# One streaming-encoder layer on one core: five reorderings of loads, sums and the final normalisation

## The chip, the cores and the metric

The kernel runs on one core of a Trainium2 chip. The metric is device time in microseconds (us); before the change three runs gave 1188.85, 1189.27 and 1189.97, median 1189.27.

## The reference, cut to what matters

For x of shape (1024, 2048), all in float32:

```
h    = rmsnorm(x) * norm_g
proj = h @ w_in                                  # 2048 x 5120
ya   = gelu(ua) * (W_s layernorm(gelu(va)) + b)  # chunked spatial gating
yb   = windowed attention(q, k, v) with sinks and relative bias
yc   = (trailing mean of 2/4/8/16 tokens - token) @ w_pool * c_scale
mix  = [ya*silu(ga), yb*silu(gb), yc*silu(gc)]
out  = rmsnorm(x + mix @ w_out) * final_g
```

## The kernel before, in words

**Tiling.** Both projections are cut into seven products of 1024 output columns, called pairs: five on w_in (PAIR_F, TA, TB, C, A, numbers 0 to 4) and two on w_out (PAIR_O, PAIR_U, 5 and 6). Each pair is computed by a Strassen-like scheme of seven block products of 512 rows by 1024 inner by 512 columns; each product takes two steps, c = 0 and 1. There are 98 steps, numbered 0 to 97. Steps 70 to 77 alternate between the pairs: O, O, U, U, O, O, U, U. Steps 78 to 87 are the rest of O and 88 to 97 the rest of U.

**One step.** TensorE multiplies 48 times, 128x128 by 128x512: four PSUM banks (st = 0 to 3), four operand slots (k = 0 to 3), and three matmuls each, because every float32 operand is split into a high and a low part in the fast float32r format (`three`). The high part of a weight tile is a ScalarE copy (`split_hi`), the low part a VectorE subtraction (`split_lo`), both one step ahead: while TensorE is in step J (we call that period J) these engines split the weights of step J + 1. VectorE also forms the sums of weight blocks (`weight_sum`), adds PSUM banks to the result quadrants (`add_chain`), and does what the layer needs between.

**Order.** Each engine runs a loop over the steps that is written out by hand, and inside an iteration strictly in order of the text. Engines meet at semaphores. SyncE (SP) issues nearly all DMAs; its iteration n does the stores of sums (`save_jobs`), weight loads (`pair_loads`), then the four slot loads of step n + 2 (`load_s`), each behind the release of its slot, then `result_loads` (mixed values, residual rows). All of SP's DMAs are on one queue. GpSimd issues, on its own queue, the saves of the first pair's operand splits (`save_first`, steps 6 to 13), on whose landing the slot loads of step 14 wait.

**Row tiles.** `ROWS_LOADED` says in which iteration one of eight 1 MB tiles of x is loaded, for the sums of squares that ScalarE takes one iteration later (`square_rows`). For an iteration below 12 the load stands ahead of `load_s(n + 2)`, from 12 on behind it. The split of weights is the first thing in ScalarE's iteration, `square_rows` nearly the last.

**Pooling.** In periods 55 to 63 VectorE's `pool_half(u)` computes a trailing mean into the tile `aux` (signal `pool_in`), TensorE's `pool_map(u)` multiplies it into the PSUM bank E[1] behind the first bank of step 56 + u, and `pool_gate(u)` empties that bank (`c_done`). `pool_map(u)` waits for `pool_half(u)` and for `pool_gate(u - 1)`.

**The end.** `finish_first` (one function on ScalarE, one on VectorE) takes the root of the first 512 rows' mean squares and scales their four 1 MB result tiles, eight instructions on each engine. SP then stores the four tiles (line 890) in iteration 96, which it reaches after the last slot loads. In the same iteration, ahead of these stores, `result_loads` loads the last 1 MB of residual rows (line 833) into the one buffer `residual`. In period 97 VectorE adds it (`add_residual`, line 1629), and only behind that, in its program order, come the last bank additions, squares, roots and scalings of the second 512 rows, and their stores (lines 896, 902 and 943).

```
if J == step(PAIR_O + 1, 12):       # = 96, the last thing of the iteration
    finish_first()
```

Of the kernel before, what the change touches and what calls it, by code (L numbers as in the profile page):

```python
# [8 lines left out]
ALU = mybir.AluOpType  # L9
# [27 lines left out]
CHUNKS = PAIRS * STEPS  # L37
# [18 lines left out]
def step(p, g):  # L56

    return 2 * SEQUENCE.index((p, g // 2)) + g % 2
# [100 lines left out]


ROW_TILES = HALVES * ST
ROWS_LOADED = {5: 0, 6: 1, 7: 2, 9: 3, 10: 4, 11: 5, 13: 6, 15: 7}
AT_ROOT = (11, 17)
AT_ROWS = (13, 19)
AT_KV = (13, 18)
# [89 lines left out]
def build(nc, x, x_t, w_b, norm_g, ln_g, ln_b, w_s, b_s, sinks, rel_bias, one_hot, inv_count, w_pool,  # L255
# [8 lines left out]
    with ExitStack() as ctx:  # L264
# [276 lines left out]
        def _(sp):  # L541
# [143 lines left out]
            def pair_loads(n):  # L685

                p, j = at_step(n)
                first, second, third = BUFS[p]
                following = p + 1 < PAIRS
                if n == step(PAIR_O, 0) - 1:  # L690
                    split_done(n + 1)
                    load_w(BUFS[PAIR_O][0], PAIR_U, B21, 0)
                for c in range(2):
                    if p == PAIR_F:
                        if j == c:
                            split_done(2 + c)
                            load_w(second, p, B22, c)
                        if j == 7 + c:
                            sums_done(p, 5 + c)
                            load_w(first, p, B22, c)  # L700
                            split_done(8 + c)
                            load_w(third, p, B21, c)
                        if j == 9 + c:
                            split_done(10 + c)
                            load_w(first, p + 1, FIRST_BLOCKS[p + 1][1], c)
                        if j == 11 + c:
                            sums_done(p, 7 + c)
                            load_w(third, p + 1, FIRST_BLOCKS[p + 1][0], c)
                        if j == 12 + c:
                            split_done(n)  # L710
                            load_w(second, p + 1, FIRST_BLOCKS[p + 1][2], c)
                    elif p == PAIR_O:
                        if j == 0 and c == 1:
                            split_done(n + 1)
                            load_w(first, PAIR_U, B21, c)
                        if j == 2 + c:
                            split_done(n)
                            sums_done(p, 1 + c)
                            load_w(second, p, B22, c)
                        if j == 6 + c:  # L720
                            split_done(n)
                            load_w(third, p, B12, c)
                        if j == 9 + c:
                            sums_done(p, 5 + c)
                            load_w(second, p, B21, c)
                        if j == 10 + c:
                            split_done(n)
                            load_w(third, PAIR_U, B12, c)
                        if j == 11 + c:
                            sums_done(p, 7 + c)  # L730
                            load_w(second, PAIR_U, B11, c)
                        if j == 12 + c:
                            split_done(n)
                            load_w(first, PAIR_U, B22, c)
                    elif p == PAIR_U:
                        if j == c:
                            split_done(n)
                            load_w(first, p, B11, c)
                        if j == 6 + c:
                            split_done(n)  # L740
                            load_w(third, p, B12, c)
                        if j == 9 + c:
                            sums_done(p, 5 + c)
                            load_w(first, p, B21, c)
                    elif early(p):
                        if j == c:
                            split_done(n)
                            load_w(first, p, B22, c)
                        if j == 6 + c:
                            split_done(n)  # L750
                            load_w(third, p, B12, c)
                        if j == 9 + c:
                            sums_done(p, 5 + c)
                            load_w(first, p, B21, c)
                        if following and j == 10 + c:
                            split_done(n)
                            load_w(third, p + 1, FIRST_BLOCKS[p + 1][0], c)
                        if following and j == 11 + c:
                            sums_done(p, 7 + c)
                            load_w(first, p + 1, FIRST_BLOCKS[p + 1][1], c)  # L760
                        if following and j == 12 + c:
                            split_done(n)
                            load_w(second, p + 1, FIRST_BLOCKS[p + 1][2], c)
                    else:
                        if j == 8 + c:
                            split_done(n)
                            load_w(third, p, B21, c)
                        if following and j == 6 + c:
                            split_done(n)
                            load_w(second, p + 1, FIRST_BLOCKS[p + 1][0], c)  # L770
                        if following and j == 11 + c:
                            sums_done(p, 7 + c)
                            load_w(third, p + 1, FIRST_BLOCKS[p + 1][1], c)
                        if following and j == 12 + c:
                            split_done(n)
                            load_w(first, p + 1, FIRST_BLOCKS[p + 1][2], c)
# [71 lines left out]
            for n in range(CHUNKS):  # L848
# [33 lines left out]
                if n == AT_LAYER:  # L882
                    load_layer_constants()
                result_loads(n)
                if n == CHUNKS - 2:

                    for c, y, done, count in ((0, y11[PAIR_O], y_scaled, 4), (1, y12[PAIR_O], y_scaled, 8),
                                              (2, y11[PAIR_O + 1], y_normed, 4), (3, y12[PAIR_O + 1], y_normed, 8)):
                        sp.wait_ge(done, count)
                        sp.dma_start(out[0:HS, 512 * c:512 * c + 512].rearrange("(t r) d -> r t d", t=ST), y[:]  # L890
                                     ).then_inc(y_stored, 16)
# [56 lines left out]
        def _(sc):  # L948
# [300 lines left out]
            for J in range(TOTAL):  # L1249
# [3 lines left out]
                if J == 0:  # L1253
                    for k in range(4):
                        first_hi(1, k)
                        split_hi(1, (k,))
                elif J + 1 < TOTAL and J not in SUM_S3:
                    split_hi(J + 1)
                if 0 < J < STEPS - 1:
                    first_hi(J + 1, 0)  # L1260
                    if J in SUM_S3:
# [46 lines left out]
                    square_rows(ROWS_LOADED[J - 1])  # L1308
                if j == 2 * EARLY.index(Q_S2) + 1 and early(p) and p > PAIR_F:
                    copy_u(p, range(ST - 1))  # L1310
                if J == step(PAIR_O + 1, 12):
                    finish_first()
            last_square(0)
            last_square(1)
            second_root(0, 2, 2)
# [14 lines left out]
        def _(ve):  # L1330
# [141 lines left out]
            def weight_sums(n):  # L1472
# [9 lines left out]
                    if j in (11, 12):  # L1482
                        weight_sum(p, j - 4, j - 11, 1, 2, 1, ALU.subtract, (2, 2))
                elif p == PAIR_O:
                    if j == 1:
                        weight_sum(p, 1, 0, 2, 2, 1, ALU.subtract, (1, 1), (2, 1))
                    if j in (8, 9):
                        weight_sum(p, j - 3, j - 8, 2, 1, 2, ALU.subtract, (2, 2))
                    if j in (10, 11):
# [3 lines left out]
                    if j == 13:  # L1493
                        weight_sum(PAIR_U, 3, 1, 2, 2, 1, ALU.subtract, (1, 4), (2, 3))
                elif p == PAIR_U:
                    if j == 0:
                        weight_sum(PAIR_O, 2, 1, 2, 2, 1, ALU.subtract, (1, 1), (2, 1))
                    if j in (2, 3):
                        ve.wait_ge(lo_done, split_index(n, 1) + 1)
                        weight_sum(PAIR_O, j + 1, j - 2, 0, 1, 2, ALU.subtract, (1, 2))  # L1500
# [148 lines left out]
            def pool_half(u):  # L1649
# [6 lines left out]
                settle(ve.tensor_copy(pool_x[:, 0:HIST], hist[:, j, :]))  # L1656
                settle(ve.tensor_tensor(pool_x[:, HIST:HIST + HS], pool_src[half][:, j, :], rstd_row[half][:], ALU.mult))
                settle(ve.tensor_copy(hist[:, j, :], pool_x[:, HS:HS + HIST]))
                if u >= 1:
                    ve.wait_ge(pool_ready, u)  # L1660
                window = POOLS[j]
                src = pool_x
                for m in range(j + 1):
                    lo, by, dst = 2 ** (m + 1) - 1, 2 ** m, (pool_a, pool_b)[m % 2]
                    settle(ve.tensor_tensor(dst[:, lo:HIST + HS], src[:, lo:HIST + HS],
                                            src[:, lo - by:HIST + HS - by], ALU.add))
                    src = dst
                last = ve.scalar_tensor_tensor(out=aux[:], in0=src[:, HIST:HIST + HS], scalar=1.0 / window,
                                               in1=pool_x[:, HIST:HIST + HS], op0=ALU.mult, op1=ALU.subtract)
                if half == 0:  # L1670
# [101 lines left out]
            for n in range(CHUNKS):  # L1772
# [41 lines left out]
                    weight_sum(PAIR_U, 4, 1, 1, 0, 2, ALU.subtract, (0, 4))  # L1814
                if STEPS <= J + 1 < TOTAL:
                    split_lo(J + 1)
                if J in PIECE_OF and PIECE_OF[J] % 2 == 0:
                    query_lo(PIECE_OF[J])
                for k, gate in enumerate(GATES):
# [34 lines left out]
                    previous_values()  # L1854

                u = J - POOL_AT
                if 0 <= u < 8:
                    pool_gate(u)
                if 0 <= u + 1 < 8:
                    pool_half(u + 1)  # L1860
                if J == step(PAIR_A, 7):
                    ve.wait_ge(mixed_loaded[0], 16 * 4)
                    ve.wait_ge(y_gated, 7)
# [21 lines left out]
                for i, t in enumerate((step(PAIR_O, 8), step(PAIR_O, 11), step(PAIR_O, 13), step(PAIR_U, 5),  # L1885
                                       step(PAIR_U, 6), step(PAIR_U, 10))):
                    if J == t:
                        weigh(i)
                if J == step(PAIR_O + 1, 12):
                    finish_first()  # L1890

            add_chain(PAIRS - 1, Q_A22, (0, 1))
            second_root(0, 2, 2)
# [322 lines left out]
```

## Time and profile before

| | |
|---|---|
| median of three runs | 1189.27 us |
| profiled execution, device time | 1189.71 us |
| its span, first to last instruction | 1187.9 us |
| busy: TensorE / VectorE / ScalarE / GpSimd | 98% / 73% / 41% / 3% |
| moved by DMA | 355 MB, mean 299 GB/s |

Busy time is time in which an instruction of that engine ran. The span is the profiled execution's time less 1.8 us that lie around it. With TensorE at 98% a change can gain only in the few places where it waits, at the start, and in the 12 us after its last matmul.

### The profile page before, as it was taken

Reading aid. Unit: us, or ns where it says so; the run is one execution under the profiler, and the core shown is the slowest. Engines: PE = TensorE matmul, PEld = TensorE weight load, DVE = VectorE, ACT = ScalarE, POOL = GpSimd, SP = SyncE. Lnnn points to the kernel's source line nnn. Section 1 sums busy time; section 2 is a strip of 40 time slices with the busy share of each in tenths; the row PEclk is TensorE's granted clock in tenths of the full one; section 3 lists DMA queues with packets and bytes.
Section 4 is the critical chain, followed back from the end, with each engine's and each line's share of the span. In section 5 each row is a group of like instructions: output and inputs, shape, how many; then the busy total and the mean of one; then the engine's idle time right before and its main releaser. Section 6 shows DMA issues by size and latency. Waiting matters only on the chain.

```text
span 1187.9 us, 15646 instructions
## 1 busy us (share of the span) xinstructions
PE 1169.2 (98%) x5862; PEld 954.5 (80%) x5862; DVE 872.3 (73%) x1150; ACT 491.5 (41%) x863; POOL 37.5 (3%) x76
## 2 busy tenths in 40 slices
PE   9999999999999999999999999999999999999995
PEld 8878878888888888888888877778878888888884
DVE  5799939677777767888776797988777445586674
ACT  6375564524534333447333362423333432223235
POOL 0012100000000000000000000000000000000000
PEclk9999999999999999999999999999999999999998
DMA  9999999687864476996567686799997648896878
GB/s 349 418 375 415 394 416 346 203 308 286 320 226 160 163 268 243 347 341 202 190 231 261 206 336 232 255 323 363 420 412 302 248 175 342 321 413 226 310 280 326
DMA packets 103435, 354.98 MB, mean 299 GB/s; under 512 B 10656, under 2 KB 17856, under 8 KB 92224
## 3 DMA queue, kind: packets, MB, share of 16 engines
q1 hardware_dynamic: 98432, 336.15, 76.7%
q0 software_dynamic: 4928, 17.83, 3.7%
q8 instruction: 47, 0.77, 0.2%
q14 instruction: 28, 0.23, 0.0%
HBM read 282.37 MB, written 71.57 MB: 298 GB/s over the span
## 4 chain that ended last, share of the span: by engine, by line
PE 81%; DVE 9%; DMA 7%; issue 1%; SPq 1%; ACT 1%; POOL 0%; DVEq 0%; ACTq 0%
PE n_bank L1911 25%; PE n_bank L1912 25%; PE n_bank L1913 25%; DMA x_parts<-s_ring 3%; PE e_bank L2062 2%; DVE w_lo L1344 2%; PE t_bank L2090 2%; PE t_bank L2073 2%; DMA xc<-x_t_dram 2%; DVE w_b L1469 1%; DMA s_ring<-m_parts 1%; DMA s_ring<-x_parts 1%; DVE s_ring L1353 1%; DMA xa<-x_t_dram 1%; DVE va L1526 0%
## 5 line engine op out<-in xcount | busy, mean ns | idle before, releaser
L1006 ACT ACTIVATE w_hi<-w_b 128x1024 fp32r<-128x1024 f32 (+1 forms) x200 | 197.8, 1033 | 421.1 <-PE n_bank L1913 365.3
L1911 PE MATMUL n_bank<-s_ring,w_hi 128*128 128x512 f32 x896 | 357.5, 399 | 1.3 <-DMA s_ring<-x_parts 1.3
L1913 PE MATMUL n_bank<-s_ring,w_lo 128*128 128x512 f32 x896 | 349.0, 390 | 0.0
L1912 PE MATMUL n_bank<-s_ring,w_hi 128*128 128x512 f32 x896 | 349.0, 389 | 0.0
L1344 DVE TENSOR_TENSOR w_lo<-w_b,w_hi 128x1024 fp32r<-128x1024 f32 (+1 forms) x200 | 231.9, 1198 | 102.9 <-ACT w_hi L1006 102.7
L1911 PE MATMUL n_bank<-w_hi,s_ring 128*128 128x512 f32 x672 | 262.1, 390 | 2.0 <-DMA s_ring<-m_parts 0.9
L1913 PE MATMUL n_bank<-w_hi,s_ring 128*128 128x512 f32 x672 | 261.5, 389 | 0.0
L1912 PE MATMUL n_bank<-w_lo,s_ring 128*128 128x512 f32 x672 | 261.5, 389 | 0.0
L1911 PEld LDWEIGHTS n_bank<-s_ring,w_hi 128*128 128x128 f32 x896 | 168.2, 188 | 41.7 <-issue 2.5
L1913 PEld LDWEIGHTS n_bank<-s_ring,w_lo 128*128 128x128 f32 x896 | 168.2, 188 | 35.7
L1912 PEld LDWEIGHTS n_bank<-s_ring,w_hi 128*128 128x128 f32 x896 | 168.3, 188 | 35.3 <-issue 2.2
L1911 PEld LDWEIGHTS n_bank<-w_hi,s_ring 128*128 128x128 f32 x672 | 126.1, 188 | 30.9 <-DMA s_ring<-m_parts 2.4
L1913 PEld LDWEIGHTS n_bank<-w_hi,s_ring 128*128 128x128 f32 x672 | 126.1, 188 | 26.1
L1912 PEld LDWEIGHTS n_bank<-w_lo,s_ring 128*128 128x128 f32 x672 | 126.1, 188 | 25.9
L1469 DVE TENSOR_TENSOR w_b<-w_b,w_b 128x2048 f32<-128x2048 f32 x56 | 127.9, 2285 | 3.9 <-DMA w_b<-w_b_dram 3.7
L1701 DVE SCALAR_TENSOR_TENSOR probs<-e_bank,score_scale,bias 64x256 f32<-64x256 f32 x128 | 56.4, 481 | 81.0 <-PE e_bank L2062 80.6
L1240 ACT ACTIVATE probs<-probs,minus_max 128x129 f32<-128x129 f32 x128 | 50.0, 393 | 51.7 <-DVE minus_max L1712 51.7
L937 POOL COPY probs<-sink_sb 128x4 f32<-128x4 f32 x32 | 17.3, 540 | 517.9 <-ACT probs L1240 412.8
L1526 DVE TENSOR_TENSOR o<-n_bank,o 128x512 f32<-128x512 f32 x32 | 20.9, 686 | 16.5 <-PE n_bank L1913 16.0
L1526 DVE TENSOR_TENSOR u<-n_bank,u 128x512 f32<-128x512 f32 x32 | 21.0, 687 | 14.1 <-PE n_bank L1913 13.8
L2090 PEld LDWEIGHTS t_bank<-probs_t,v_prev 128*64 128x64 f32 x256 | 14.7, 136 | 11.7 <-issue 11.7
L1240 ACT ACTIVATION_READ_ACCUMULATOR probs<-probs,minus_max 128x1 f32 x128 | 23.9, 187 | 0.0
(210 smaller groups left out, 945.3 us busy)
## 6 DMA issues: line engine op xcount, KB each, us to landing
s_ring<-x_parts SPq DMA_DIRECT2D x224, 512.0 KB, 6.0
w_b<-w_b_dram SPq DMA_DIRECT2D x76, 1024.0 KB, 10.6
s_ring<-m_parts SPq DMA_DIRECT2D x96, 512.0 KB, 6.1
x_parts<-s_ring POOLq DMA_DIRECT2D x32, 512.0 KB, 11.4
x_parts<-s_ring SPq DMA_DIRECT2D x24, 512.0 KB, 14.5
m_parts<-stage SPq DMA_DIRECT2D x20, 512.0 KB, 8.6
rows<-x_dram SPq DMA_DIRECT2D x8, 1024.0 KB, 11.3
residual<-x_dram SPq DMA_DIRECT2D x6, 1024.0 KB, 9.5
```

Of the source, the lines that this page charges most:

```text
L1006: sc.activation(w_hi[:, J % 2, part], w_source(J)[:, part], ACT.Copy).then_inc(hi_done, 1)
L1240: sc.activation(part, part, ACT.Exp, bias=minus_max[:, b:b + 1], accum_out=row_sum[:, b:b + 1]).then_inc(exp_done, 1)
L1344: ve.tensor_tensor(w_lo[:, J % 2, part], w_source(J)[:, part], w_hi[:, J % 2, part].bitcast(F32), ALU.subtract).then_inc(lo_done, 1)
L1469: ve.tensor_tensor(out[:], a[:], b[:], op).then_inc(w_summed, 1)
L1526: ve.tensor_tensor(out[:, st, :], N[st][:], to[:, st, :], ALU.add).then_inc(y_added, 1)
L1701: last = ve.scalar_tensor_tensor(out=logits[rows, 2 * tl:2 * tl + 2, 0:P], in0=e_banks[rows, :, at:at + P], scalar=score_scale[rows, half, ...
L1911: pe.matmul(psum_out, stat[0], mov[0], start=first, stop=False)
L1912: pe.matmul(psum_out, stat[0], mov[1], start=False, stop=False)
L1913: return pe.matmul(psum_out, stat[1], mov[0], start=False, stop=last)
L2062: mm = pe.matmul(E[a][:, 256 * tl:256 * tl + WINDOW], q_part[rows, at:at + P], k_part[rows, q0:q0 + WINDOW], start=k == 0, stop=k == 2)
L2073: mm = pe.transpose(PT_bank[:, P * b:P * b + P], logits[:, b, 0:P], ident[:])
L2090: mm = pe.matmul(O_bank[64 * a:64 * a + 64, P * tl + 64 * c:P * tl + 64 * c + 64], vals[:, st, d], probs_t[:, at + 64 * c:at + 64 * c + 64 ...
```

## The change

There are five edits:

1. Row tile 5 is loaded in iteration 12 instead of 11, so behind the slot loads of step 14; its squares move from ScalarE's period 12 to 13.
2. The third weight block of PAIR_O (2 x 1 MB) is loaded in iterations 71 and 72 instead of 68 and 69.
3. The weight sum that uses it moves from periods 71 and 72 to 73 and 74.
4. `pool_half(u + 1)` stands ahead of `pool_gate(u)`, and its wait for `pool_ready` stands just ahead of the instruction that overwrites `aux`.
5. `finish_first` moves from the end of period 96 to period 95, right behind the split of step 96's weights, on both engines; the four stores move from SP's iteration 96 to 95.

```diff
-ROWS_LOADED = {5: 0, 6: 1, 7: 2, 9: 3, 10: 4, 11: 5, 13: 6, 15: 7}
+ROWS_LOADED = {5: 0, 6: 1, 7: 2, 9: 3, 10: 4, 12: 5, 13: 6, 15: 7}
@@ pair_loads, p == PAIR_O
+                        if j == 1 and c == 0:
+                            split_done(n)
+                            load_w(third, p, B12, c)
@@ pair_loads, p == PAIR_U
+                        if j == 0 and c == 1:
+                            split_done(n)
+                            load_w(third, PAIR_O, B12, c)
@@ pair_loads, early(p)
-                        if following and j == 12 + c:
+                        if following and p < PAIR_A and j == 12 + c:
                             split_done(n)
                             load_w(second, p + 1, FIRST_BLOCKS[p + 1][2], c)
@@ sync, behind result_loads(n)
-                if n == CHUNKS - 2:
+                if n == CHUNKS - 3:
...
@@ scalar, behind split_hi(J + 1)
+                if J == step(PAIR_U, 11):
+                    finish_first()
@@ scalar, end of the iteration
-                if J == step(PAIR_O + 1, 12):
-                    finish_first()
@@ weight_sums
                 elif p == PAIR_O:
-                    if j == 1:
-                        weight_sum(p, 1, 0, 2, 2, 1, ALU.subtract, (1, 1), (2, 1))
+                    if j == 2:
+                        weight_sum(p, 2, 1, 2, 2, 1, ALU.subtract, (1, 1), (2, 1))
                 elif p == PAIR_U:
-                    if j == 0:
-                        weight_sum(PAIR_O, 2, 1, 2, 2, 1, ALU.subtract, (1, 1), (2, 1))
+                    if j == 1:
+                        weight_sum(PAIR_O, 1, 0, 2, 2, 1, ALU.subtract, (1, 1), (2, 1))
@@ pool_half
-                if u >= 1:
-                    ve.wait_ge(pool_ready, u)
...
+                if u >= 1:
+                    ve.wait_ge(pool_ready, u)
                 last = ve.scalar_tensor_tensor(out=aux[:], ...)
@@ vector, behind split_lo(J + 1)
+                if J == step(PAIR_U, 11):
+                    finish_first()
@@ vector
+                if 0 <= u + 1 < 8:
+                    pool_half(u + 1)
                 if 0 <= u < 8:
                     pool_gate(u)
-                if 0 <= u + 1 < 8:
-                    pool_half(u + 1)
@@ vector, end of the iteration
-                if J == step(PAIR_O + 1, 12):
-                    finish_first()
```

## Rows read from the trace of the kernel before

**Rows 1.** Page: busy time, and the chain that ended last, by engine.

```profile
PE 1169.2 (98%) x5862; PEld 954.5 (80%) x5862; DVE 872.3 (73%) x1150; ACT 491.5 (41%) x863; POOL 37.5 (3%) x76
PE 81%; DVE 9%; DMA 7%; issue 1%; SPq 1%; ACT 1%; POOL 0%; DVEq 0%; ACTq 0%
```

**Rows 2.** Busy time by stretch: length, engines, granted clock, DMA share, GB/s.

```profile
162.11:176.08 13.97, 12.70 (x58) 9.76 (x57) 6.45 (x13) 3.87 (x5) 0.00 (x0) 1.00 1.02 415
742.17:753.96 11.79, 11.79 (x52) 9.39 (x50) 10.78 (x14) 4.62 (x7) 0.00 (x0) 1.00 0.90 313
753.96:767.00 13.04, 12.03 (x52) 9.31 (x50) 12.70 (x20) 4.79 (x5) 0.00 (x0) 1.00 0.48 164
767.00:779.80 12.80, 12.18 (x52) 9.13 (x50) 12.39 (x22) 3.08 (x5) 0.00 (x0) 1.00 0.78 287
868.78:879.66 10.88, 10.88 (x49) 8.92 (x48) 8.90 (x8) 5.21 (x4) 0.00 (x0) 1.00 1.03 420
879.66:892.37 12.71, 11.77 (x49) 8.78 (x49) 7.43 (x8) 2.53 (x3) 0.00 (x0) 1.00 1.03 406
1163.20:1187.20 24.00, 12.21 (x54) 9.76 (x53) 11.95 (x21) 11.41 (x24) 2.18 (x4) 0.80 0.95 350
```

**Rows 3.** Chain of waits inside step 14: start, us, what.

```profile
156.43 9.83 DMA s_ring<-x_parts
...
175.45 0.87 PE t_bank L1939 x8
```

**Rows 4.** Waits of TensorE over the span: us in total, times, longest.

```profile
PE e_bank L2120 <- DVE aux L1674: 1.6, 2, 1.0
```

**Rows 5.** DMAs issued from 867 to 869 us, the slots of step 71.

```profile
s_ring<-m_parts SPq DMA_DIRECT2D x4, 512.0 KB, 13.4
```

**Rows 6.** Tile out_dram, issues from 1163 to 1168 us: issue ns, landing us.

```profile
L890 SPq DMA_DIRECT2D out_dram<-o x2: 378/384/389, 1163.3 to 1165.7; - x2
L890 SPq DMA_DIRECT2D out_dram<-u x2: 568/940/1312, 1166.1 to 1166.8; - x2
...
DMA to landing us min/median/max: 4.3/5.8/9.1
```

**Rows 7.** DMAs issued from 134.5 to 138.5 us: size, median us to landing.

```profile
x_parts<-s_ring POOLq DMA_DIRECT2D x4, 512.0 KB, 17.8
```

**Rows 8.** Timeline of ScalarE: start, us, instruction, idle before it and releaser.

```profile
176.39 1.92 ACT L1048 ACTIVATE rows<-rows 128x2048 f32<-128x2048 f32 x1 [6.76 <-DMA rows<-x_dram]
```

**Rows 9.** Timeline of VectorE from period 95 to the end.

```profile
1148.56 3.70 DVE L1526 TENSOR_TENSOR u<-n_bank,u 128x512 f32<-128x512 f32 x6
...
1155.90 2.35 DVE L1344 TENSOR_TENSOR w_lo<-w_b,w_hi 128x1024 fp32r<-128x1024 f32 x2
1158.16 0.16 DVE L1740 TENSOR_REDUCE ssq_sum<-ssq 128x4 f32<-128x16 f32 x1
...
1160.67 3.26 DVE L1747 TENSOR_SCALAR u<-u,rstd_y 128x512 f32<-128x512 f32 x8
1163.85 2.28 DVE L1629 TENSOR_TENSOR u<-u,residual 128x2048 f32<-128x2048 f32 x1
...
1168.53 0.16 DVE L1753 TENSOR_REDUCE ssq_sum<-ssq 128x2 f32<-128x8 f32 x1 [1.08 <-ACT e_bank L956]
...
1169.26 2.74 DVE L1761 SCALAR_TENSOR_TENSOR u<-u,rstd_y,final_g_sb 128x512 f32<-128x512 f32 x4
```

**Rows 10.** Timeline of SP's DMA issues at the end.

```profile
1151.64 2.36 SPq L672 DMA_DIRECT2D s_ring<-m_parts  x4
1154.68 0.38 SPq L833 DMA_DIRECT2D residual<-x_dram  x1
...
1171.36 1.69 SPq L896 DMA_DIRECT2D out_dram<-u  x2
```

**Rows 11.** The last slot load, issued at 1153.68 us.

```profile
s_ring<-m_parts SPq DMA_DIRECT2D x1, 512.0 KB, 6.3
```

**Rows 12.** The last residual load, issued at 1154.68 us.

```profile
residual<-x_dram SPq DMA_DIRECT2D x1, 1024.0 KB, 7.9
```

## The prediction

> **What bounds the kernel now.** I first read the page's busy times and its chain: TensorE is busy for 98% of the span and holds 81% of the chain [rows 1]. So a transfer or a VectorE instruction is worth something only where TensorE waits for it, or behind TensorE's last matmul. I then cut the span into steps. A step without a wait takes 10.88 us, as step 70 does, and one with a pooling map 11.79 us, as step 59 does [rows 2]. Against these the longer ones show the price of each wait; the waits of TensorE name the releasers, but split the time between matmuls and weight loads, so I take prices from the step lengths.
>
> Step 14 takes 13.97 us. 10.88 are its matmuls and 0.87 the eight transposes at its end [rows 2, 3]; of the other 2.22 I put 0.4 down to the start behind a plain float32 matmul and 1.8 to slots that landed late. The chain shows the last of these: issued at 156.43, landed 9.83 us later at 166.26, when TensorE wanted it near 164.2 [rows 3]. Steps 60 and 61, with pooling, are 13.04 - 11.79 = 1.25 and 12.80 - 11.79 = 1.01 too long, and the releaser is the last instruction of `pool_half` [rows 2, 4]. Step 71 is 12.71 - 10.88 = 1.83 too long; its slots took a median 13.4 us to land [rows 2, 5].
>
> Behind the matmuls the end belongs to the DMA engines, which the engine chain alone hides. From 1163.2 to 1187.2 us their share is 0.95 [rows 2]. The first 1 MB store is issued at 1163.3 and lands 4.3 us later, at 1167.6; the fourth at 1166.8, and lands 9.1 later, at 1175.9 [rows 6]. So a megabyte passes in (1175.9 - 1167.6)/3 = 2.77 us behind a latency of 4.3 - 2.77 = 1.5. Eight of them from 1163.3 give 1163.3 + 1.5 + 22.2 = 1187.0, and the span ends at 1187.9: the stores pass without a gap, and 0.9 us close the program.
>
> **Edit 1, the row tile.** In the step before and in step 14 the DMA engines are full (share 1.02, 415 GB/s, so 2.5 us a megabyte) [rows 2]. The slot loads of step 14 wait for GpSimd's four saves of step 12, which take 17.8 us to land [rows 7]. One megabyte less ahead of them is up to 2.5 us. The moved load itself now stands in SP's queue behind the four slot loads and ahead of the next weight block and of step 15's slots; the bytes ahead of those are what they were. ScalarE now stands in period 13 before row tile 5 until it lands, near 166.5 (one megabyte, 2.5 us, behind slots that end near 164), then squares for 2.1 us, and queued behind it are the split of step 15's weights, 2.0 us on ScalarE and 2.4 on VectorE, done by about 172; TensorE wants them at 176.08 - 1.8 = 174.3. That is covered by 2 us, and if the tile landed 3 us later than I think, each further microsecond would cost one. After it ScalarE waits for row tile 6 until 176.39 as before [rows 8], so its lateness ends there. Bounds: +1 us (the cover fails) and -1.8 us (all of the wait). I take -1.8, since 2.5 us are more than the 2.1 by which the last slot was late.
>
> The Trainium skill (DMA: Bandwidth & Descriptors, "Queues, rings and completion order") says that each DMA engine takes turns between the queues that have work, a packet at a time. By that rule the saves on GpSimd's queue get their share whatever waits in SP's, so that a shorter SP queue doesn't speed them until it is empty; if SP's queue never emptied, edit 1 would give nothing and the forecast would be 1.8 us higher. No row ahead shows the turns themselves.
>
> **Edits 2 and 3, the weight block.** Two megabytes leave the queue ahead of step 71's slots; at a share of 1.03 and 420 GB/s [rows 2] they are 2 x 2.5 = 5.0 us, more than the 1.83 that step 71 lost. They return in iterations 71 and 72, in which SP loads no slots because steps 72 and 73 find theirs in place, so nothing urgent is queued behind them; the residual rows behind them are wanted only in period 73. The sums (2.3 us each) move to periods 73 and 74. VectorE has some 9 us of work in periods such as 70 (8.90 of 10.88) [rows 2] and the sum's reader is step 80. Bounds: -1.83 and +1 (a late addition in period 73 or 74). I take -1.8, the whole wait.
>
> **Edit 4, the pooling.** Steps 60 and 61 wait because VectorE is full: 12.70 of 13.04 and 12.39 of 12.80 us [rows 2]. `pool_map(u + 1)` waits for both `pool_half(u + 1)` and `pool_gate(u)`. Before, gate then half; after, half then gate: the later of the two ends at the same time, as the same instructions run in a different order. The wait that moves was long over when VectorE came to it. Before, TensorE was released by the end of the half, line 1674 [rows 4]; after, it will be the end of the gate, at the same place. Bounds: -2.26 (both excesses, if the gate were not waited for) and +0.3 (a longer last instruction). I take 0, because no idle time of VectorE is used.
>
> **Edit 5, the normalisation and its stores.** On VectorE `finish_first` is a sum, a reciprocal and eight scalings, 3.26 us [rows 9]. The lead costs 0.7 us where the root's table is in place (1168.53 to 1169.26 for the second half's), and 2.5 us where it isn't (1158.16 to 1160.67) [rows 9]; ScalarE is idle in period 95 and can load the table ahead of its wait, so I take 0.7. These 4.0 us now stand ahead of a weight sum, six bank additions, a residual addition and the split of step 97's weights. The first two of the six additions (0.62 each) free the first bank; they end at 1149.8 + 4.0 = 1153.8, and TensorE wants the bank when step 95 ends, at 1153.5 (the last slot load, which waits for that, is issued at 1153.7 [rows 10]): 0.3 us. The split of step 97's weights starts at 1155.90 + 4.0, its first half ends 1.2 later at 1161.1; TensorE wants it half a step into 96, at 1153.8 + 5.4 = 1159.2: 1.9 us [rows 9]. So TensorE ends 2.2 us later; with the longer lead of 2.5 us it would be 4.0. That cover was `finish_first`'s old place, where nothing of TensorE's stood behind it.
>
> The larger effect is in SP's queue. The four stores are ready by about 1152, so SP issues them from 1154.0, straight behind the last slot loads [rows 10]. The last residual load, which stood ahead of them and was issued at 1154.68, now stands behind four megabytes. The slots end at 1153.68 + 6.3 = 1160.0, and the residual landed at 1154.68 + 7.9 = 1162.6 [rows 11, 12], that is 2.6 us of transfer. Now: 1160.0 + 4 x 2.77 + 2.6 = 1173.7. VectorE's `add_residual` started at 1163.85 and would start at 1173.7, 9.8 us later, and queued behind it on VectorE are all of the second half's additions, roots and scalings. The 2.2 us of TensorE vanish beneath this. From its start to the first of the second half's stores it was 1171.36 - 1163.85 = 7.5 us [rows 9, 10]: now 1181.2. From then on four megabytes are left: 1181.2 + 1.5 + 4 x 2.77 = 1193.8, against 1187.0. So edit 5 costs 6.8 us. The bounds are -2.3 us (worked out below, if the load isn't late) and +9.8 us (if all the lateness reaches the end). I take 6.8, because half of the stores' backlog is gone and pays back 3 of the 9.8.
>
> **The sum.** Against the profiled execution: 1189.71 - 1.8 - 1.8 + 0 + 6.8 = 1192.9. That execution is 0.44 above the median of the runs, so against 1189.27 I forecast 1192.5 us, slower by 3.2 us or 0.27%.
>
> **Rivals.** First, faster: the residual load is not held up (the DMA engines serve it beside the stores, so that it lands near 1164 to 1166). Then the stores' backlog is what went: TensorE ends at 1175.4 + 2.2, the second half's stores begin at 1171.4 + 0.7, and the end is 1172.1 + 1.5 + 11.1 = 1184.7 against 1187.0, that is -2.3; sum 1189.27 - 3.6 - 2.3 = 1183.4. For it speaks that the engines' share of 0.95 leaves a little room and that no row shows a load behind stores of this shape; against it, that the residual landed right behind the slots, 2.6 us for its megabyte, as in one line. It decides from a landing before about 1169. Second, between: the load is held up by half, the addition starts near 1169, and the end moves by about +2; 1187.7. Third, steps 14 and 71 stay as long (the transfers are only late elsewhere, or ScalarE's wait for row tile 5 reaches TensorE) while edit 5 costs what I say: 1189.27 + 6.8 = 1196.1. For it: the bytes in the full stretches are the same. Fourth, the pooling gains its 2.3 us after all: 1190.2.
>
> **Chances.** The forecast has 0.55, the faster rival 0.22, the one between 0.08, the third 0.08, the fourth 0.07. About 0.2% (2.4 us) is what a measurement of this kernel can tell from no change, so faster is below 1186.9 and slower above 1191.7. The forecast lies only 0.8 us above that bound; I give 0.43 of its 0.55 to slower and 0.12 to the same. Slower is then 0.43 + 0.08 = 0.51, the same 0.12 + 0.08 + 0.07 = 0.27, faster 0.22. The forecast's own range is 1190 to 1195. The range for 8 in 10 takes in the rivals between and fourth and reaches toward both others: 1186.0 to 1196.5.
>
> **What would show it.** Step 14 should be near 12.2 us and step 71 10.9; the row tile should land near 166.5 and ScalarE should stand before it about 5 us. Steps 60 and 61 should keep their 13.0 and 12.8, with TensorE released by line 1682 instead of 1674. Step 96 and 97 together should be about 2 us longer. The last residual load should take some 14 us or more to land, VectorE should be idle for about 10 us ahead of line 1629, and the last store should land some 18 us behind TensorE's last matmul. I am wrong if that addition starts within 3 us of the split ahead of it; then the time is below 1187.

## The result, and the profile after

The changed kernel takes 1194.08 us (median of five runs, 1193.47 to 1194.44) against 1188.94 for the kernel before on the same chip: a ratio of 1.0045, 95% interval [1.0033, 1.0057]. That is 5.1 us slower. The forecast was 1192.5, slower by 3.2. The spans of the two profiled executions differ by 1192.3 - 1187.9 = 4.4 us.

The page of the changed kernel, where the chain is to be set against [rows 1]:

```profile
span 1192.3 us, 15649 instructions
PE 86%; DVE 7%; DMA 3%; SPq 2%; issue 1%; ACT 1%; POOL 0%; DVEq 0%; ACTq 0%
```

The shares of the whole say little. The steps do: busy time by stretch, columns as in [rows 2], for steps 14, 60, 61, 71 and 96 of the changed kernel.

```profile
162.10:174.29 12.19, 12.19 (x58) 9.93 (x57) 5.67 (x11) 5.67 (x6) 0.00 (x0) 1.00 1.01 417
752.23:765.44 13.21, 11.95 (x52) 9.27 (x50) 12.90 (x19) 4.83 (x6) 0.00 (x0) 1.00 0.47 160
765.44:778.23 12.79, 12.12 (x52) 9.17 (x50) 12.41 (x22) 3.03 (x5) 0.00 (x0) 1.00 0.79 288
878.06:888.94 10.88, 10.88 (x50) 9.01 (x48) 5.81 (x7) 2.53 (x3) 0.00 (x0) 1.00 1.02 408
1150.39:1163.28 12.89, 11.29 (x49) 9.04 (x49) 8.18 (x9) 4.83 (x10) 0.00 (x0) 1.00 0.97 355
```

Steps 14 and 71 hold no wait any more: TensorE is busy for the whole 12.19 and the whole 10.88 us. Steps 60 and 61 are where they were, the first even 0.2 longer. Step 96 is 2.0 us longer than a plain one. The waits of TensorE over the span name the releasers in steps 60, 61 and 96 (compare [rows 4]):

```profile
PE e_bank L2126 <- DVE tc L1688: 1.9, 2, 1.3
PE n_bank L1917 <- DVE w_lo L1350: 1.6, 1, 1.6
```

Line 1688 is the end of `pool_gate` in the changed kernel, line 1350 the split of weights. The larger effect is in SP's queue. Its issues at the end (compare [rows 10]):

```profile
1150.61 1.00 SPq L896 DMA_DIRECT2D out_dram<-o  x2
1151.66 5.13 SPq L896 DMA_DIRECT2D out_dram<-u  x2
1156.83 2.39 SPq L839 DMA_DIRECT2D residual<-x_dram  x1
1178.45 1.03 SPq L902 DMA_DIRECT2D out_dram<-u  x2
```

and VectorE's timeline of the same stretch (compare [rows 9]):

```profile
1143.55 3.26 DVE L1753 TENSOR_SCALAR u<-u,rstd_y 128x512 f32<-128x512 f32 x8
...
1156.36 2.35 DVE L1350 TENSOR_TENSOR w_lo<-w_b,w_hi 128x1024 fp32r<-128x1024 f32 x2
1170.93 2.29 DVE L1635 TENSOR_TENSOR u<-u,residual 128x2048 f32<-128x2048 f32 x1 [12.22 <-DMA residual<-x_dram]
```

VectorE sits idle for 12.22 us in front of `add_residual`, until the last megabyte of residual rows has landed. The chain of waits of the changed kernel runs through the same two things, a store whose issue holds SP for 4.12 us, and the load behind it:

```profile
1152.67 4.12 SPq L896
1156.83 14.07 DMA residual<-x_dram
1170.93 2.30 DVE u L1635
```

### The profile page after: what moved, and what is told of

Read it like the earlier page. It is cut to its first block, busy times and chain, and to the rows that moved or that the text cites. A ratio compares the mean times of both kernels' runs of the same rounds, so it can differ in the third digit from the quotient of the medians.

```text
span 1192.3 us, 15649 instructions
## 1 busy us (share of the span) xinstructions
PE 1167.5 (98%) x5862; PEld 953.7 (80%) x5862; DVE 871.8 (73%) x1150; ACT 491.0 (41%) x863; POOL 37.5 (3%) x76
## 4 chain that ended last, share of the span: by engine, by line
PE 86%; DVE 7%; DMA 3%; SPq 2%; issue 1%; ACT 1%; POOL 0%; DVEq 0%; ACTq 0%
PE n_bank L1917 27%; PE n_bank L1919 26%; PE n_bank L1918 26%; PE e_bank L2068 2%; PE t_bank L2096 2%; PE t_bank L2079 2%; DMA xc<-x_t_dram 1%; DVE w_lo L1350 1%; DMA residual<-x_dram 1%; DVE w_b L1475 1%; SPq L562 1%; DMA xa<-x_t_dram 1%; SPq L896 1%; PE e_bank L2114 0%; DVE s_ring L1361 0%
## 5 line engine op out<-in xcount | busy, mean ns | idle before, releaser
L943 POOL COPY probs<-sink_sb 128x4 f32<-128x4 f32 x32 | 17.3, 539 | 519.7 <-ACT probs L1246 412.3
L1532 DVE TENSOR_TENSOR o<-n_bank,o 128x512 f32<-128x512 f32 x32 | 20.9, 686 | 16.9 <-PE n_bank L1919 16.8
```

Of the source, the lines that this page charges most:

```text
L1532: ve.tensor_tensor(out[:, st, :], N[st][:], to[:, st, :], ALU.add).then_inc(y_added, 1)
```

## The experiments

Two theories were to be told apart. **Q**: edit 5 costs what it does because the residual load stands behind four stores in SP's queue. **V**: it costs because VectorE's scalings stand ahead of the work that TensorE waits for. On these chips the kernel before ran at 1188.5 us.

| kernel | median us | ratio to before, 95% | span |
|---|---|---|---|
| e1_without_edit5: edits 1 to 4 | 1186.29 | 0.9981 [0.9972, 0.9989] | 1184.5 |
| e2_edit5_alone | 1196.58 | 1.0066 [1.0053, 1.0078] | 1195.2 |
| e3_load_before_stores | 1185.65 | 0.9977 [0.9968, 0.9986] | 1183.6 |
| e4_root_early_scale_late | 1183.23 | 0.9955 [0.9942, 0.9969] | 1181.7 |
| e5_two_stores_ahead | 1189.11 | 1.0005 [0.9995, 1.0014] | 1187.9 |
| e6_load_behind_stores | 1201.45 | 1.0106 [1.0092, 1.0120] | 1200.1 |
| e7_sum_job_early | 1186.61 | 0.9981 [0.9972, 0.9990] | 1185.4 |
| e8_all_gains | 1181.86 | 0.9942 [0.9929, 0.9954] | 1179.8 |

**Everything but edit 5.** The changed kernel with both `finish_first` and the four stores back in their old places.

```diff
-                if n == CHUNKS - 3:
+                if n == CHUNKS - 2:
@@ scalar, vector
-                if J == step(PAIR_U, 11):
+                if J == step(PAIR_O + 1, 12):
                     finish_first()
```

> Edits 1 to 4 without edit 5. Both theories: steps 14 and 71 lose 1.8 us each (12.2 and 10.9 us long), steps 60 and 61 stay at 13.0 to 13.3 and 12.8, and the end is as before. Time 1188.9 - 3.4 = 1185.5 us; above 1187 would mean that the gains in the middle are not kept to the end.

Measured 1186.29, so the changed kernel loses 1194.08 - 1186.29 = 7.8 us by edit 5, and by the spans 1192.3 - 1184.5 = 7.8 as well. Edits 1 to 4 together gain 2.2 us, where 3.4 were expected; most of the shortfall is edit 1, whose price is taken up below.

**Edit 5 alone.** The same lines the other way round, on the kernel before.

```diff
-                if n == CHUNKS - 2:
+                if n == CHUNKS - 3:
@@ scalar, vector
-                if J == step(PAIR_O + 1, 12):
+                if J == step(PAIR_U, 11):
                     finish_first()
```

> Edit 5 alone on the kernel before. Theory Q (the last residual load stands behind four stores in SP's queue): about +8 us, 1197 us, the residual load lands 14 us after its issue and VectorE idles 11 to 12 us ahead of the residual addition. Theory V (the cost is the four microseconds of scalings that now stand ahead of TensorE's weights on VectorE): the end is late by the 2 us that TensorE loses, 1191 us, and the addition follows the split directly.

Measured 1196.58, 8.1 us more than before; Q's number, not V's. The waits of VectorE in this kernel from 1140 us on (us in total, times, longest):

```profile
DVE u L1629 <- DMA residual<-x_dram: 12.2, 1, 12.2
```

**The load ahead of the stores.** One number in the changed kernel: the four stores go back to iteration 96, where they stand behind `result_loads`; the early normalisation stays.

```diff
-                if n == CHUNKS - 3:
+                if n == CHUNKS - 2:
```

> All five edits, but the four stores stay in SP's iteration 96, so behind the residual load; finish_first stays in period 95. Theory Q: the residual lands by 1161 us, VectorE's addition follows the split of step 97's weights at once, TensorE still ends 2 us late, and the stores' backlog is shorter: 1188.9 - 3.4 - 2.3 = 1183.2 us. Theory V: the scalings still stand ahead of the weights, so most of the loss stays, 1190 us or more.

Measured 1185.65: 8.4 us come back by the order of five DMAs alone, with VectorE's instructions as in the changed kernel. That settles it for Q: V's cost is there, but it lies hidden beneath Q's. VectorE's timeline now has 2.62 us in place of 12.22:

```profile
1155.70 2.35 DVE L1350 TENSOR_TENSOR w_lo<-w_b,w_hi 128x1024 fp32r<-128x1024 f32 x2
1160.67 2.29 DVE L1635 TENSOR_TENSOR u<-u,residual 128x2048 f32<-128x2048 f32 x1 [2.62 <-DMA residual<-x_dram]
```

But its median is only 0.6 us below that of e1, whose runs (1185.67 to 1186.50) all lie inside the range of its own (1185.15 to 1186.65), and it missed its expectation by 2.4. Step 96 is still long, for TensorE waits for the split of weights as in the changed kernel:

```profile
1149.72:1162.60 12.88, 11.27 (x48) 9.05 (x49) 10.12 (x10) 4.84 (x10) 0.00 (x0) 1.00 0.91 311
```

**Root early, scalings late.** What of VectorE is worth having early? Here period 95 keeps the sum, the root, the reciprocal and ScalarE's eight scalings; VectorE's eight go back to the end of period 96. The stores stand as in e3, and edit 4 is undone.

```diff
                 ve.wait_ge(y_root, 1)
                 ve.reciprocal(rstd_y[0][:], root_y[0][:]).then_inc(y_inverted, 1)
+            def scale_first():
+                ve.wait_ge(y_inverted, 1)
+                ve.wait_ge(y_weighed, 6)
                 for y in (y11[PAIR_O + 1], y12[PAIR_O + 1]):
...
+                if J == step(PAIR_O + 1, 12):
+                    scale_first()
```

> Edits 1 to 3; in period 95 only the sum, the root, the reciprocal and ScalarE's eight scalings; VectorE's eight scalings in period 96 where they were; stores in iteration 96 behind the residual load. TensorE loses nothing in steps 96 and 97 (0.9 us more on VectorE are covered by the 2 us by which the split of step 97's weights was early), two stores leave near 1152 us, two near 1160. Theory Q: the stores of the second half follow without a gap, 1188.9 - 3.4 - 2.3 = 1183.2 us, the same as with all of finish_first early, because the stores set the end in both. If TensorE's 2 us set the end, this one is 2 us faster than the other.

Measured 1183.23, and 2.4 us faster than e3. That is the second branch of the expectation: TensorE's 2 us set the end. The agreement with 1183.2 is in part luck: that number was worked out for the first branch, in which both kernels would have been equal; edits 1 to 3 gave less than its 3.4 us, and the end gave more than its 2.3. Some 0.2 of the difference to e3 is edit 4 (below). The step 96 of e4 and VectorE's timeline:

```profile
1150.10:1161.00 10.90, 10.90 (x50) 9.01 (x48) 9.72 (x14) 4.79 (x10) 0.00 (x0) 1.00 0.99 355
```

```profile
1155.38 3.25 DVE L1756 TENSOR_SCALAR u<-u,rstd_y 128x512 f32<-128x512 f32 x8
1159.77 2.29 DVE L1635 TENSOR_TENSOR u<-u,residual 128x2048 f32<-128x2048 f32 x1 [1.14 <-DMA residual<-x_dram]
```

The step is back at 10.9 with ScalarE's eight scalings still early, so it was VectorE's eight that cost TensorE its 2 us. What both kernels have in common is the end: the last store lands 9.3 us behind the start of the last matmul in e3 (1173.26, 1182.56) and 9.0 in e4 (1171.65, 1180.69), and 12.1 in e1 (1171.61, 1183.67). In all three the last store of GpSimd is issued 5.1 us behind that start (1178.33, 1176.73 and 1176.68). What differs is how long the last stores then take to land. GpSimd's four, in e1, in e3 and in e4:

```profile
out_dram<-o POOLq DMA_DIRECT2D x4, 256.0 KB, 6.3
```

```profile
out_dram<-o POOLq DMA_DIRECT2D x4, 256.0 KB, 4.0
```

```profile
out_dram<-o POOLq DMA_DIRECT2D x4, 256.0 KB, 3.7
```

In e1 they still queue behind the stores ahead of them. With most of that backlog gone the end follows TensorE, and V's 2 us count in full.

**Two stores ahead.** A dose between: two of the four stores stay in iteration 95, two follow the residual load in 96.

```diff
-                result_loads(n)
-                if n == CHUNKS - 3:
+                if n in (CHUNKS - 3, CHUNKS - 2):
...
-                                              (2, y11[PAIR_O + 1], y_normed, 4), (3, y12[PAIR_O + 1], y_normed, 8)):
+                                               ((2, y11[PAIR_O + 1], y_normed, 4), (3, y12[PAIR_O + 1], y_normed, 8))
+                                              )[n - (CHUNKS - 3)]:
```

> The changed kernel with only two of the four stores in SP's iteration 95; the other two follow the residual load in iteration 96. Theory Q prices each store ahead of the load at 2.7 us: the load lands 2 x 2.7 us earlier than with four ahead, near 165.4 + 1000 us instead of 1170.9, and since the stores of the second half then run with no gap behind, the end moves by the same 5.4 us: 1194.1 - 5.5 = 1188.6 us. Theory V: no difference from the changed kernel, 1194 us.

Measured 1189.11, 0.5 above Q's number and 5 below V's; the idle time in front of `add_residual` is between those of e3 and the changed kernel:

```profile
DVE u L1636 <- DMA residual<-x_dram: 7.3, 1, 7.3
```

**The order alone, on the kernel before.** Nothing is normalised early; in iteration 96 the residual load is merely issued behind the four stores.

```diff
-                result_loads(n)
+                if n != CHUNKS - 2:
+                    result_loads(n)
...
                 if n == CHUNKS - 2:
...
+                    result_loads(n)
```

> The kernel before with one exchange: in SP's iteration 96 the four stores stand ahead of the residual load; finish_first stays in period 96. TensorE, VectorE and ScalarE have the order of before. Theory Q: the stores go at 1163.3 as before, end at 1175.9, and the load behind them lands at 1178.5 instead of 1162.6; the addition starts 14.7 us later; the first of the second half's stores is issued at 1178.5 + 7.5 = 1186, the last lands at 1186 + 1.5 + 11.1 = 1198.6, so the time is 1188.5 + 11.6 = 1200 us. Theory V: no scaling was moved, so within 1 us of before.

Measured 1201.45, slower by 13 us, with no scaling moved. VectorE's waits and the chain of this kernel:

```profile
DVE u L1631 <- DMA residual<-x_dram: 15.4, 1, 15.4
```

```profile
1167.48 11.21 DMA residual<-x_dram
1178.69 0.02 issue
1178.72 2.30 DVE u L1631
```

Part of the lateness here is a wait in SP (the stores themselves are ready only from 1162.6), not transfer. Yet the four kernels in which the load is late obey one line: the span ends 21.4 us behind its landing.

| kernel | residual landed | span | difference |
|---|---|---|---|
| two stores ahead (e5) | 1166.53 | 1187.9 | 21.4 |
| changed kernel | 1170.90 | 1192.3 | 21.4 |
| edit 5 alone (e2) | 1173.8 | 1195.2 | 21.4 |
| order alone (e6) | 1178.69 | 1200.1 | 21.4 |

**The pooling's real cover.** Steps 60 and 61 wait since VectorE is full in them, so here a job leaves them: the kernel before with one sum of operands, which stood in period 58, one period earlier.

```diff
-(s2(44), "s", 3, (0, 1))
+(s2(43), "s", 3, (0, 1))
```

> The kernel before with one job of VectorE (the seven instructions, 5 us, that form and split the sums of the last attention tiles) moved from period 58 to 57, where VectorE has idle time. If steps 60 and 61 wait because VectorE is full from period 58 to 61, both come down to 11.8 us: 1188.5 - 2.2 = 1186.3 us. If they wait for the map's own chain of half and gate, whose order edit 4 exchanged, they stay at 13.0 and 12.8 us and the time with them.

Measured 1186.61. Steps 60 and 61 lose their excess, VectorE now busy for 11.01 and 11.45 of 11.79 us. But step 59, which took 11.79 before [rows 2], now takes 12.46. The stretches of steps 59, 60 and 61:

```profile
741.47:753.93 12.46, 12.02 (x51) 9.31 (x50) 12.05 (x18) 3.81 (x5) 0.00 (x0) 1.00 0.47 172
753.93:765.72 11.79, 11.79 (x51) 9.39 (x50) 11.01 (x17) 5.97 (x7) 0.00 (x0) 1.00 0.52 179
765.72:777.51 11.79, 11.79 (x52) 9.39 (x50) 11.45 (x21) 2.46 (x3) 0.00 (x0) 1.00 0.86 311
```

In step 59 TensorE now waits for the end of `pool_half`:

```profile
PE e_bank L2120 <- DVE aux L1668: 0.4, 1, 0.4
```

So part of VectorE's backlog is only pushed into the step ahead: of the 2.3 us of excess, 1.6 are gained over the three steps (13.04 + 12.80 + 11.79 before, 12.46 + 11.79 + 11.79 now), and 1.8 by the medians.

**All gains.** Edits 1 to 3, the end of e4 and the job of e7.

> Edits 1 to 3, the early root with VectorE's scalings in period 96, the residual load ahead of the stores, and the job in period 57; edit 4 undone. The gains lie at different places and should add: 1183.2 - 2.2 = 1181.0 us, steps 14, 60, 61 and 71 at 12.2, 11.8, 11.8 and 10.9 us. If VectorE's backlog of period 58 is only pushed on, 1183.

Measured 1181.86, ratio 0.9942 [0.9929, 0.9954]: faster than either kernel, by 6.6 us (1188.45 - 1181.86) and by 12.2. It is 0.9 above the 1181.0 that was expected, and 0.7 of that is step 59, which takes 12.49 here too. Its steps 14, 59, 60, 61 and 71:

```profile
162.00:174.13 12.13, 12.13 (x59) 9.94 (x57) 5.76 (x12) 5.67 (x6) 0.00 (x0) 1.00 1.01 415
740.22:752.71 12.49, 12.05 (x51) 9.31 (x50) 12.07 (x18) 3.80 (x5) 0.00 (x0) 1.00 0.48 170
752.71:764.50 11.79, 11.79 (x52) 9.39 (x50) 10.99 (x16) 5.96 (x7) 0.00 (x0) 1.00 0.49 174
764.50:776.28 11.78, 11.78 (x51) 9.38 (x50) 11.44 (x21) 2.46 (x3) 0.00 (x0) 1.00 0.84 315
876.02:886.90 10.88, 10.88 (x50) 9.01 (x48) 5.05 (x7) 2.53 (x3) 0.00 (x0) 1.00 1.00 402
```

## Why the prediction was right, and where its sizes were off

The sign, the place and the mechanism were right: three small edits give a little, and edit 5 takes more than they give, through the queue. The size was 1.9 us short, 5.1 against 3.2, and no error hid another: all the misses point the same way. By term:

| term | predicted | measured | from |
|---|---|---|---|
| edit 1 | -1.8 | -1.8 in the shown execution, about -0.9 otherwise | step 14 |
| edits 2 and 3 | -1.8 | -1.8 | step 71 |
| edit 4 | 0 | +0.2 | steps 60, 61 together |
| edit 5 | +6.8 | +7.8 | changed kernel less e1 |

**Edit 1: right in kind, its price taken from an unlucky execution.** GpSimd's saves of step 12 land sooner. DMAs issued from 135 to 138.5 us in the changed kernel, where [rows 7] had 17.8 (and e2, e6 and e7, without edit 1, had 17.1, 17.3 and 16.9):

```profile
x_parts<-s_ring POOLq DMA_DIRECT2D x4, 512.0 KB, 15.1
```

ScalarE's wait for the row tile came out as forecast, 5 us until about 166, and no delay of TensorE followed:

```profile
165.95 1.92 ACT L1054 ACTIVATE rows<-rows 128x2048 f32<-128x2048 f32 x1 [5.02 <-DMA rows<-x_dram]
```

The rule of turns between queues (Trainium skill, DMA: Bandwidth & Descriptors, "Queues, rings and completion order") was read as a warning that the saves would not gain; that outcome did not come, since the saves landed sooner and the wait in step 14 is gone. Whether the engines take turns packet by packet no run here shows. But e2, e6 and e7 hold edit 1's code as before, and in their profiled executions step 14 took 13.06, 13.02 and 13.12 us, not 13.97. The stretch in e2, in e6 and in e7:

```profile
162.43:175.49 13.06, 12.43 (x58) 9.83 (x57) 6.45 (x13) 3.87 (x5) 0.00 (x0) 1.00 1.02 417
```

```profile
161.95:174.97 13.02, 12.67 (x59) 9.76 (x57) 6.45 (x13) 3.86 (x5) 0.00 (x0) 1.00 1.02 417
```

```profile
162.25:175.37 13.12, 12.43 (x58) 9.76 (x57) 6.44 (x13) 3.87 (x5) 0.00 (x0) 1.00 1.02 416
```

So the 1.8 us that [rows 2] showed were some 0.9 above what the other executions lose there. The changed kernel took 12.19 and e8, with edit 1 too, 12.13. With -0.9 for edit 1 the terms add up to -0.9 - 1.8 + 0.2 + 7.8 = +5.3 us, against +5.1 by the medians of the first comparison; with -1.8 they give the +4.4 of the spans. This is one of the two mis-sized terms.

**Edits 2 and 3: right.** Step 71's slots, issued from 865 to 867.6 us in the changed kernel, against the 13.4 of [rows 5]:

```profile
s_ring<-m_parts SPq DMA_DIRECT2D x4, 512.0 KB, 8.5
```

The step is at 10.88, and no step from 72 to 94 is longer than before: the load and the sums found room in their new places.

**Edit 4: nearly right.** The releaser changed from the end of the half to the end of the gate and the time stayed but for an extra 0.2 us, inside the bound of 0.3. The reason given, no idle time of VectorE is used, fits e7: taking work out of the full periods helps, less what the period that takes it loses.

**Edit 5: right, 1.0 us short.** Moved to the changed kernel's times (its last slot load is issued at 1150.25, 3.43 earlier than before) the working gave 1150.25 + 6.3 + 4 x 2.77 + 2.6 = 1170.2 for the landing of the residual rows; it was 1170.90. The four stores and the load themselves took 13.5 us behind the last slot, where 13.7 were predicted, but the last slot took 7.1 us and not 6.3. Behind the landing the prediction had 7.5 + 1.5 + 11.1 + 0.9 = 21.0 us, and 21.4 were measured. TensorE's +2.2 came too (0.3 at step 96's start and 2.0 inside it), hidden as predicted: the last store landed at 1191.23, 16.9 us behind the end of the last matmul (1174.32). The sign named in advance was some 18, but the prediction's own terms give 1193.8 - 1177.6 = 16.2. The lead of the scalings was 0.7 us as taken (1142.81 to 1143.55), for ScalarE loaded the root's table while it would have waited:

```profile
1141.46 1.28 ACT L977 ACT_TABLE_LOAD   x1
```

The 2.5 us of [rows 9], with which this was compared, were not the table's alone: 1.28 were the load, and before it ScalarE was busy with squares until 1158.8.

**The rivals.** The faster one needed the residual load in time; e3 builds that case, and its price was wrong. The prediction gave the tail -2.3 us; e3 less e1 is -0.6. It had counted only the bytes that are left to store, but with the backlog gone the end lies 9.3 us behind the start of TensorE's last matmul, which was at 1175.0 before: 1175.0 + 2.2 + 9.3 + 0.9 = 1187.4, half a microsecond below the 1187.9 of before. The rival between (the load held up by half) is e5: landed at 1166.5, at 1189.1 us. The third is out by step 71; the fourth by steps 60 and 61.

## What to carry to other kernels

A store that becomes ready early is not free to issue early: on a queue with a backlog it takes its whole transfer from every load behind it, here 2.7 us per megabyte, so put the last load that an engine still needs ahead of all stores, and then let the stores go. When bringing work forward, bring only the part that releases others (here the root and the scalings of the idle engine) and leave the rest where nothing waits behind it. When a job is moved out of a full period, look at the period that takes it as well: e7 gained 2.3 us in two steps and lost 0.7 in a third. And price a stall that hangs on the landing of DMAs from more than one execution, for one may show twice the usual loss.

## What the runs showed of the hardware that was not expected

**An issue can hold SP itself for microseconds.** With three slot loads and three stores not yet landed, the fourth store took 4.12 us to issue and the load behind it 2.39, where the load took 0.38 in e3. The two stores of `u` in the changed kernel (issue ns, minimum, median, maximum):

```profile
L896 SPq DMA_DIRECT2D out_dram<-u x2: 961/2542/4123, 1151.7 to 1152.7; - x2
```

The number of transfers not yet landed doesn't set this alone. In e3 the fourth store found the load and three stores outstanding and took 2.66 us; in e4 it found the same and took 0.42, but there SP had paused for 3.5 us after the second store. What sets it stays open. It cost nothing here, as the load would have stood in the queue instead. The load waits for its one buffer, which VectorE's addition gave back at 1152.83 + 2.29 = 1155.12, and SP came to it at 1156.83, so its 14.1 us to landing leave out 1.7 us of lateness. A DMA's time to landing understates how late it is; its place in the order of issues tells more.

**Loads and stores landed in one line.** In the changed kernel the five transfers landed one by one in their order, at 1159.9, 1162.5, 1165.1, 1168.3 and 1170.9, steps of 2.6 to 3.2 us, although four write to memory and the fifth reads. The four stores count on one semaphore, so their times say when its counts were full and their order among themselves is taken from the issues; that the load came last is measured, on a semaphore of its own.
